# Attention over the prompt: where the next keys stand between the scores and the turn of two other heads

## The chip, the core and the metric

The kernel runs on one core of a Trainium2 chip. The metric is the device time of one execution in microseconds. A core has a matrix engine (TensorE, PE in the rows; its loads of weights are listed apart as PEld), a vector engine (VectorE, DVE), a scalar engine (ScalarE, ACT), GpSimd (POOL) and SyncE (SP), which here issues nearly all transfers. Each engine works through its own queue in order, and the engines wait for each other on semaphores.

## What is computed

One step of a two-layer streaming encoder trunk over a prompt of 256 frames and 8 running streams of 16 frames each. Layer 0 mixes by multi-head latent attention, layer 1 by retention; each has a half feed-forward block before and behind. The change lies in the attention of layer 0 over the prompt, 8 heads:

```python
def mla_prompt(h, pos, w_dq, q_norm, w_uq, w_dkv, kv_norm, w_uk, w_uv, w_o):
    q_nope, q_pe, ckv, kpe = mla_project(...)
    k_nope = jnp.einsum('bkl,lhn->bkhn', ckv, w_uk)          # keys
    v = jnp.einsum('bkl,lhv->bkhv', ckv, w_uv)               # values
    for blk in range(s // QBLK):                             # 2 blocks of 128 queries
        q0 = blk * QBLK
        kend = q0 + QBLK
        sc = (jnp.einsum('bqhn,bkhn->bhqk', q_nope[:, q0:kend], k_nope[:, :kend])
              + jnp.einsum('bqhr,bkr->bhqk', q_pe[:, q0:kend], kpe[:, :kend]))
        ...
        p = jax.nn.softmax(jnp.where(mask, sc, -jnp.inf), axis=-1).astype(v.dtype)
        outs.append(jnp.einsum('bhqk,bkhv->bqhv', p, v[:, :kend]))
```

## The kernel before, in words

The program is a row of phases: feed-forward, attention, feed-forward, feed-forward, retention, feed-forward, end. The feed-forward blocks and projections multiply in three terms with weights split into a high and a low part (L167 to L169); they hold most of the time.

In the attention phase the prompt part is written out by hand, once for each engine. What sets the order is only the order of the calls in `pe_prompt` (TensorE) and `act` (ScalarE), and what `dve` does per head; semaphores then hold an engine at the head of its queue. For head h the steps are:

- `keys(h)`: TensorE, two products into a bank (L928); ScalarE copies them to `kn` (L1150), two buffers.
- `scores(h)`: TensorE, four products into bank `up_ps[h % 2]` (L944, L945), for two blocks of 128 queries with 128 and 256 keys.
- VectorE takes the row maxima (L1322) and negates them (L1326); ScalarE's `exps(h)` writes `pr` (L1171, in the rows `cc`, whose memory it shares); VectorE inverts the sums (L1333) and scales `pr` (L1338).
- `turn(h)`: TensorE, three transposes of `pr` into `down_ps[h % 2]` (L956); ScalarE's `turned(h)` copies them to `prT` (L1162, in the rows `mtab`).
- `mix(h)`: TensorE, values by `prT` (L969), which waits for that copy; ScalarE's `mixed(h)` copies the result to `XH` (L1154), and VectorE keeps the rest in `XL` (L1312).
- `sample_queries(n)`, n = 0 to 3: TensorE, eight small products for the running streams (L985); ScalarE copies each to `lat` in two instructions (L1141).

In the steady loop TensorE works through turn(h), keys(h+3), mix(h), scores(h+2), turn(h+1), and so on. ScalarE's queue is keys, mixed, turned, exps in each pass. In the passes i = 2 and 3 ScalarE and VectorE also split a half of a weight tile (L152, L160). Behind the prompt part comes that of the running streams (`sample_scores`, L1035 and L1039, and `pe_sample`), and then the output projection.

Of the kernel before, what the change touches and what calls it, by code (L numbers as in the profile page):

```python
# [15 lines left out]
MLA_HEADS, NOPE, ROPE, Q_LORA, KV_LORA = D_MODEL // 128, 128, 64, 3 * D_MODEL // 8, D_MODEL // 4  # L16
# [30 lines left out]
def stream_kernel(nc, a, out):  # L47

    ctx = ExitStack()
    with ctx:  # L50
# [13 lines left out]
        def sem(name):  # L64

            if name not in sems:
                sems[name] = ctx.enter_context(nc.semaphore(name))
            return sems[name]
# [684 lines left out]
        class Mla:  # L753
# [146 lines left out]
            def pe_prompt(self, pe):  # L900
# [3 lines left out]
                def values(i):  # L904
                    kt_, half = i // 2, i % 2
                    if i >= 2:
                        pe.wait_ge(sem("m_proj"), (15, 18)[i - 2])
                    for t in range(KV):
                        pe.wait_ge(sem("m_ckvT"), t + 1)
                        mm = pe.matmul(self.VAL_BANKS[i][:, 0:512], ckvT[:, t, kt_ * P:(kt_ + 1) * P],  # L910
                                       wuv[:, t, half * 512:(half + 1) * 512], start=(t == 0), stop=(t == KV - 1))
                    mm.then_inc(sem("m_val"), 1)
# [7 lines left out]
                def keys(h):  # L920
                    if h == 0:
                        pe.wait_ge(sem("wuk_in"), 16)
                    if h < 2:
                        pe.wait_ge(sem("m_proj"), (13, 16)[h])
                    else:
                        pe.wait_ge(sem("m_kn"), h - 1)
                    for t in range(KV):
                        mm = pe.matmul(gate_ps[1 - h % 2][:, 0:SEQ], wuk[:, t, h * P:(h + 1) * P], ckvT[:, t, 0:SEQ],  # L928
                                       start=(t == 0), stop=(t == KV - 1))
                    mm.then_inc(sem("m_keys"), 1)  # L930

                def scores(h):
                    pe.wait_ge(sem("m_kn"), h + 1)
                    if h % 2 == 0:
                        pe.wait_ge(sem("m_rope"), 3 + 3 * (h // 2 + 1))
                    if h < 2:
                        pe.wait_ge(sem("m_proj"), (17, 14)[h])
                    else:
                        pe.wait_ge(sem("m_exp"), 2 * (h - 1))
                    ps = up_ps[h % 2]  # L940
                    at = 0
                    for blk in range(NP):
                        n, q0 = (blk + 1) * QBLK, blk * QBLK
                        pe.matmul(ps[:, at:at + n], qn[:, h, q0:q0 + QBLK], kn[:, h % 2, 0:n], start=True, stop=False)  # L944
                        mm = pe.matmul(ps[:, at:at + n], qp[:, h, q0:q0 + QBLK], kpT[:, 0:n], start=False, stop=True)  # L945
                        at += n
                    mm.then_inc(sem("m_scores"), 1)

                def turn(h):
                    pe.wait_ge(sem("m_pr"), 2 * (h + 1))  # L950
                    if h < 2:
                        pe.wait_ge(sem("m_val_out"), (4, 3)[h])
                    else:
                        pe.wait_ge(sem("m_prT"), h - 1)
                    for i in range(SC // P):
                        mm = pe.transpose(down_ps[h % 2][:, i * P:(i + 1) * P], pr[:, h % 2, i * P:(i + 1) * P], ident[:, :])  # L956
                    mm.then_inc(sem("m_prTurned"), 1)

                def mix(h):
                    ps = (norm_ps, misc_ps)[h % 2]  # L960
                    pe.wait_ge(sem("m_prT"), h + 1)
                    if h == 0:
                        pe.wait_ge(sem("m_val_out"), 4)
                    if h >= 2:
                        pe.wait_ge(sem("m_ol"), h - 1)
                    at = 0
                    for blk in range(NP):
                        for k in range(blk + 1):
                            mm = pe.matmul(ps[:, blk * QBLK:(blk + 1) * QBLK], val[:, k, h * P:(h + 1) * P],  # L969
                                           prT[:, h % 2, at:at + P], start=(k == 0), stop=(k == blk))  # L970
                            at += P
                    mm.then_inc(sem("m_mixed"), 1)

                def sample_queries(i):

                    ps = gate_ps[i % 2]
                    if i == 0:
                        pe.wait_ge(sem("m_kn"), MLA_HEADS)
                        pe.wait_ge(sem("wukT_in"), 16)
                    if i >= 2:  # L980
                        pe.wait_ge(sem("m_lat"), KV * (i - 1))
                    for t in range(KV):
                        for e in range(2):
                            h = 2 * i + e
                            mm = pe.matmul(ps[:, (t * 2 + e) * P:(t * 2 + e + 1) * P], wukT[:, h, t * P:(t + 1) * P],  # L985
                                           qn[:, h, SEQ:T], start=True, stop=True)
                    mm.then_inc(sem("m_qlat"), 1)
# [5 lines left out]
                keys(1)  # L993
                scores(0)
                values(3)
                for i in range(2, MLA_HEADS + 1):
                    if i < MLA_HEADS:
                        keys(i)
                    else:
                        sample_queries(0)  # L1000
                        sample_queries(1)
                    if i >= 3:
                        mix(i - 3)
                    scores(i - 1)
                    turn(i - 2)
                sample_queries(2)
                sample_queries(3)
                mix(MLA_HEADS - 2)
                turn(MLA_HEADS - 1)
                self.sample_scores(pe, 0)  # L1010
# [81 lines left out]
            def act(self, act):  # L1092
# [35 lines left out]
                def value_tile(i):  # L1128
                    act.wait_ge(sem("m_val"), i + 1)
                    act.activation(val[:, i // 2, (i % 2) * 512:(i % 2 + 1) * 512], self.VAL_BANKS[i][:, :], ACT.Copy)\  # L1130
                        .then_inc(sem("m_val_out"), 1)
# [5 lines left out]
                def sample_queries(i):  # L1137
                    act.wait_ge(sem("m_qlat"), i + 1)
                    ps = gate_ps[i % 2]
                    for t in range(KV):  # L1140
                        act.activation(lat[:, t, :, 2 * i:2 * i + 2, :].rearrange("p b e q -> p e b q"),  # L1141
                                       ps[:, t * 2 * P:(t + 1) * 2 * P].rearrange("p (e b q) -> p e b q", e=2, b=DEC_BATCH),
                                       ACT.Copy).then_inc(sem("m_lat"), 1)


                def keys(h):
                    act.wait_ge(sem("m_keys"), h + 1)
                    if h >= 2:
                        act.wait_ge(sem("m_scores"), h - 1)
                    act.activation(kn[:, h % 2, :], gate_ps[1 - h % 2][:, 0:SEQ], ACT.Copy).then_inc(sem("m_kn"), 1)  # L1150

                def mixed(h):
                    act.wait_ge(sem("m_mixed"), h + 1)
                    act.activation(XH[:, h, 0:SEQ], (norm_ps, misc_ps)[h % 2][:, 0:SEQ], ACT.Copy).then_inc(sem("m_oh"), 1)  # L1154

                def turned(h):
                    act.wait_ge(sem("m_prTurned"), h + 1)
                    if h == 0:
                        act.wait_ge(sem("m_rope"), 3 + 3 * 4)
                    if h >= 2:  # L1160
                        act.wait_ge(sem("m_mixed"), h - 1)
                    act.activation(prT[:, h % 2, :], down_ps[h % 2][:, 0:SC], ACT.Copy).then_inc(sem("m_prT"), 1)  # L1162
# [18 lines left out]
                exps(0)  # L1181
                value_tile(2)
                value_tile(3)
                for i in range(2, MLA_HEADS + 1):
                    if i < MLA_HEADS:
                        keys(i)
                    else:
                        sample_queries(0)
                        sample_queries(1)
                    if i >= 3:  # L1190
                        mixed(i - 3)
                    turned(i - 2)
                    exps(i - 1)
                    if i < 4:
                        c = self.c0 + 8
                        part_hi(act, c, c % 2, c // 2, i % 2)
                sample_queries(2)
                sample_queries(3)
                mixed(MLA_HEADS - 2)
                turned(MLA_HEADS - 1)  # L1200
                mixed(MLA_HEADS - 1)
# [968 lines left out]
```

## Time and profile before

| | |
|---|---|
| time, three runs | 1614.07 us median (1613.97 to 1615.7) |
| the profiled execution's own time | 1614.1 us |
| its span, first to last instruction | 1611.9 us |
| TensorE busy | 1601.0 us, 99% of the span |
| TensorE weight loads busy | 1535.7 us, 95% |
| VectorE busy | 822.2 us, 51% |
| ScalarE busy | 597.8 us, 37% |
| GpSimd busy | 262.7 us, 16% |
| mean granted TensorE clock | 0.999 of full speed |

A product's recorded duration overlaps that of the next, since products are pipelined: what one costs the path is the distance from its start to the start of the next. The loop that is changed runs from about 338 to 362 us of the span. Around the span lie 1614.1 - 1611.9 = 2.2 us.

### The profile page before, as it was taken

To read this page: it belongs to the slowest core of one execution; us is meant where nothing else is said; L and a number is where in the kernel's file an instruction comes from. 1 tells how busy PE (TensorE), PEld (TensorE's weight loads), DVE (VectorE), ACT (ScalarE), POOL (GpSimd) and SP (SyncE) were. 2 spreads that over 40 slices of the span, in tenths; PEclk is the share of its full clock that TensorE was granted. 3 is DMA by queue.
4 is the path that set the end of the run, shared out by engine and by line. 5 is a ranking of instruction groups with operands and counts; after the bars stand their busy time and mean duration, and the time that the engine had idled before them with its cause. 6 is when DMAs were issued, how large, how long until landed. Compare 5 with 4: busy or idle time off the path is not lost.

```text
span 1611.9 us, 24112 instructions
## 1 busy us (share of the span) xinstructions
PE 1601.0 (99%) x9170; PEld 1535.7 (95%) x9170; DVE 822.2 (51%) x968; ACT 597.8 (37%) x770; POOL 262.7 (16%) x250
## 2 busy tenths in 40 slices
PE   9999999999999999999999999999999999999998
PEld 9999999989999999999999999798989899999987
DVE  6544344864454444445444344675747486444422
ACT  6333322574343332234333323424243354333322
POOL 0111122631121110221111032202020202111000
PEclk9999999999999999999999999999999999999999
DMA  7444344554244443454444345566574755444332
GB/s 219 123 120 128 110 128 128 177 185 163 63 121 130 130 130 97 127 141 131 130 130 122 108 126 191 189 227 224 199 252 167 260 182 144 130 130 130 113 125 102
DMA packets 323440, 239.07 MB, mean 148 GB/s; under 512 B 9216, under 2 KB 287936, under 8 KB 323264
## 3 DMA queue, kind: packets, MB, share of 16 engines
q1 hardware_dynamic: 322960, 237.92, 48.3%
q8 instruction: 32, 0.52, 0.1%
q10 hardware_dynamic: 432, 0.50, 0.1%
q14 instruction: 16, 0.13, 0.0%
HBM read 215.34 MB, written 20.94 MB: 147 GB/s over the span
## 4 chain that ended last, share of the span: by engine, by line
PE 95%; SPq 2%; ACT 1%; DMA 1%; DVE 1%; issue 0%; ACTq 0%
PE bank L167 26%; PE bank L168 26%; PE bank L169 26%; PE bank L488 2%; PE bank L489 2%; PE bank L487 2%; SPq L1568 2%; PE bank L1067 1%; PE bank L396 1%; PE bank L1653 1%; PE bank L1655 1%; PE bank L1654 1%; PE bank L1763 1%; PE bank L1035 1%; PE bank L1722 1%; PE bank L1039 1%
## 5 line engine op out<-in xcount | busy, mean ns | idle before, releaser
L144 DVE TENSOR_TENSOR WL<-RAW,WH 128x2048 fp32r<-128x2048 f32 (+3 forms) x191 | 402.7, 2110 | 289.6 <-ACT WH L137 288.8
L137 ACT ACTIVATE WH<-RAW 128x2048 fp32r<-128x2048 f32 (+3 forms) x191 | 330.0, 1730 | 565.3 <-PE bank L169 478.1
L167 PE MATMUL bank<-XH,WH 128*128 128x384 f32 x1376 | 461.1, 335 | 0.0
L169 PE MATMUL bank<-XH,WL 128*128 128x384 f32 x1376 | 459.8, 334 | 0.0
L168 PE MATMUL bank<-XL,WH 128*128 128x384 f32 x1376 | 459.7, 334 | 0.0
L167 PEld LDWEIGHTS bank<-XH,WH 128*128 128x128 f32 x1376 | 258.3, 188 | 3.4 <-issue 2.0
L168 PEld LDWEIGHTS bank<-XL,WH 128*128 128x128 f32 x1376 | 258.3, 188 | 0.2
L169 PEld LDWEIGHTS bank<-XH,WL 128*128 128x128 f32 x1376 | 258.3, 188 | 0.0
L653 POOL TENSOR_TENSOR si<-si,rsb 128x384 f32<-128x384 f32 x88 | 94.7, 1076 | 625.5 <-ACT si L524 591.1
L167 PE MATMUL bank<-AH,WH 128*128 128x384 f32 x528 | 176.4, 334 | 0.0
L168 PE MATMUL bank<-AL,WH 128*128 128x384 f32 x528 | 176.4, 334 | 0.0
L169 PE MATMUL bank<-AH,WL 128*128 128x384 f32 x528 | 176.4, 334 | 0.0
L584 DVE TENSOR_TENSOR au<-bank,si 128x384 f32<-128x384 f32 x86 | 48.0, 558 | 250.0 <-PE bank L169 232.4
L524 ACT ACTIVATE si<-gs 128x384 f32<-128x384 f32 x86 | 45.2, 525 | 229.1 <-DVE gs L576 229.1
L167 PE MATMUL bank<-X2H,WH 128*128 128x384 f32 x344 | 114.9, 334 | 0.0
L169 PE MATMUL bank<-X2H,WL 128*128 128x384 f32 x344 | 114.9, 334 | 0.0
L168 PE MATMUL bank<-X2L,WH 128*128 128x384 f32 x344 | 114.9, 334 | 0.0
L167 PEld LDWEIGHTS bank<-AH,WH 128*128 128x128 f32 x528 | 99.1, 188 | 0.0
L168 PEld LDWEIGHTS bank<-AL,WH 128*128 128x128 f32 x528 | 99.1, 188 | 0.0
L169 PEld LDWEIGHTS bank<-AH,WL 128*128 128x128 f32 x528 | 99.1, 188 | 0.0
L167 PEld LDWEIGHTS bank<-X2H,WH 128*128 128x128 f32 x344 | 64.6, 188 | 0.1
L168 PEld LDWEIGHTS bank<-X2L,WH 128*128 128x128 f32 x344 | 64.6, 188 | 0.0
(282 smaller groups left out, 1938.0 us busy)
## 6 DMA issues: line engine op xcount, KB each, us to landing
RAW<-w_ffn_gate_dram SPq DMA_DIRECT2D x86, 512.0 KB, 3.9
RAW<-w_ffn_up_dram SPq DMA_DIRECT2D x86, 512.0 KB, 5.1
RAW<-w_ret_in_dram SPq DMA_DIRECT2D x48, 512.0 KB, 4.6
RAW<-w_ffn_down_dram SPq DMA_DIRECT2D x48, 384.0 KB, 4.0
st<-state_ret_dram SPq DMA_DIRECT2D x32, 512.0 KB, 6.9
new_state_sample_dram<-st SPq DMA_DIRECT2D x32, 512.0 KB, 6.5
RAW<-w_ffn_down_dram SPq DMA_DIRECT2D x48, 320.0 KB, 3.4
RAW<-w_ffn_down_dram SPq DMA_DIRECT2D x22, 512.0 KB, 3.9
```

The lines of the kernel that those rows point to most:

```text
L137: ins = act.activation(dst(WH), src, ACT.Copy)
L144: ins = dve.tensor_tensor(dst(WL), src, dst(WH).bitcast(F32), ALU.subtract)
L167: pe.matmul(ps, wh, xh, start=first, stop=False)
L168: pe.matmul(ps, wh, xl, start=False, stop=False)
L169: return pe.matmul(ps, wl, xh, start=False, stop=last)
L487: pe.matmul(ps[:, :], ah, wh, start=False, stop=False)
L488: pe.matmul(ps[:, :], ah, wl, start=False, stop=False)
L489: mm = pe.matmul(ps[:, :], al, wh, start=False, stop=(stop and f == 1))
L524: act.activation(si[:, j, :], gs[:, j, :], ACT.Silu).then_inc(self.silu_done, 1)
L584: dve.tensor_tensor(au[:, j, :], up_ps[j][:, 0:T], si[:, j, :], ALU.mult).then_inc(self.act_done, 1)
L653: pool.tensor_tensor(si[:, j, :], si[:, j, :], rsb[:, 0:T], ALU.mult).then_inc(self.silu_scaled, 1)
L1568: sp.dma_start(vp[row:row + DEC_SEQ, odd, :], src).then_inc(sem("r_vd_in"), 16)
```

## The change

In both queues the keys of head i+1 are now made in pass i, behind scores(i-1) and ahead of turn(i-2), where they had stood at the start of pass i+1, behind turn(i-2). keys(2) moves out of the loop and keeps its place. The sample queries, which take the place of the keys at the end, move in the same way: 0 and 1 go ahead of turn(5), 2 and 3 ahead of turn(6). Waits, buffers, instructions and transfers are the same; the line numbers behind the change fall by one or two.

```diff
@@ pe_prompt @@
                 scores(0)
                 values(3)
+                keys(2)
                 for i in range(2, MLA_HEADS + 1):
-                    if i < MLA_HEADS:
-                        keys(i)
-                    else:
-                        sample_queries(0)
-                        sample_queries(1)
                     if i >= 3:
                         mix(i - 3)
                     scores(i - 1)
+                    if i + 1 < MLA_HEADS:
+                        keys(i + 1)
+                    else:
+                        for n in (0, 1) if i < MLA_HEADS else (2, 3):
+                            sample_queries(n)
                     turn(i - 2)
-                sample_queries(2)
-                sample_queries(3)
                 mix(MLA_HEADS - 2)
                 turn(MLA_HEADS - 1)
@@ act @@
                 value_tile(3)
+                keys(2)
                 for i in range(2, MLA_HEADS + 1):
-                    if i < MLA_HEADS:
-                        keys(i)
-                    else:
-                        sample_queries(0)
-                        sample_queries(1)
                     if i >= 3:
                         mixed(i - 3)
+                    if i + 1 < MLA_HEADS:
+                        keys(i + 1)
+                    else:
+                        for n in (0, 1) if i < MLA_HEADS else (2, 3):
+                            sample_queries(n)
                     turned(i - 2)
                     exps(i - 1)
                     if i < 4:
                         c = self.c0 + 8
                         part_hi(act, c, c % 2, c // 2, i % 2)
-                sample_queries(2)
-                sample_queries(3)
                 mixed(MLA_HEADS - 2)
                 turned(MLA_HEADS - 1)
```

TensorE in one pass of the loop: L944 and L945 are the scores, L928 the keys, L956 the turn, L969 the mix.

```order
 L944 MATMUL bank<-kn,shared 128x256
 L945 MATMUL bank<-kall,qp 128x256
+L928 MATMUL bank<-kall,shared 128x256 x2
 L956 MATMUL bank<-ident,cc 128x128 x3
-L928 MATMUL bank<-kall,shared 128x256 x2
 L969 MATMUL bank<-mtab,val 128x128 x3
 L944 MATMUL bank<-kn,shared 128x128
```

The keys moved from behind the turn to ahead of it, so that the mix now follows the turn of the same head. Five passes look like this.

TensorE in the last pass, with the sample queries (L985) in the place of the keys:

```order
 L944 MATMUL bank<-kn,shared 128x256
 L945 MATMUL bank<-kall,qp 128x256
+L985 MATMUL bank<-shared,wukT 128x128 x8
 L956 MATMUL bank<-ident,cc 128x128 x3
-L985 MATMUL bank<-shared,wukT 128x128 x8
 L969 MATMUL bank<-mtab,val 128x128 x3
 L956 MATMUL bank<-ident,cc 128x128 x3
```

Two passes have them: turn(5) and mix(5), turn(6) and mix(6) now stand side by side, and turn(7) comes right behind mix(6).

ScalarE between two turns, before (L1171 the exponentials, L1150 the keys, L1154 the mix, L1162 the turn):

```order
L1171 ACTIVATE cc,stat<-bank,stat 128x128
L1171 ACTIVATE cc,stat<-bank,stat 128x256
L1150 ACTIVATE kn<-bank 128x256
L1154 ACTIVATE XH<-bank 128x256
L1162 ACTIVATE mtab<-bank 128x384
```

and with the change, where the same lines are one lower:

```order
L1170 ACTIVATE cc,stat<-bank,stat 128x128
L1170 ACTIVATE cc,stat<-bank,stat 128x256
L1153 ACTIVATE XH<-bank 128x256
L1149 ACTIVATE kn<-bank 128x256
L1161 ACTIVATE mtab<-bank 128x384
```

The copy of the keys now stands between the copy of the mix and that of the turn; it is that of a head one higher.

## Rows read from the trace of the kernel before

**Rows 1.** The page: the chain that ended last, shares by engine.

```profile
PE 95%; SPq 2%; ACT 1%; DMA 1%; DVE 1%; issue 0%; ACTq 0%
```

**Rows 2.** The chain between 402 and 1020 us, shares by line.

```profile
by line: PE bank L168 31.9%; PE bank L167 31.9%; PE bank L169 31.8%; PE bank L1067 0.7%; PE bank L1087 0.6%; PE bank L1653 0.5%; PE bank L1654 0.5%; PE bank L425 0.4%; PE bank L423 0.4%; PE bank L430 0.4%; PE bank L1655 0.4%; PE bank L220 0
```

**Rows 3.** TensorE timeline: start us, us, line, operands, records [idle before <-releaser].

```profile
344.76 0.49 PE L956 MATMUL bank<-ident,cc 128*128 128x128 f32 x3
345.09 1.03 PE L928 MATMUL bank<-kall,shared 128*128 128x256 f32 x4
345.95 0.83 PE L969 MATMUL bank<-mtab,val 128*128 128x128 f32 x6
346.62 0.39 PE L944 MATMUL bank<-kn,shared 128*128 128x128 f32 x2
...
347.07 0.60 PE L944 MATMUL bank<-kn,shared 128*128 128x256 f32 x2
347.50 0.59 PE L945 MATMUL bank<-kall,qp 128*128 128x256 f32 x2
348.12 0.55 PE L956 MATMUL bank<-ident,cc 128*128 128x128 f32 x3
```

**Rows 4.** TensorE timeline, around the turn of head 1.

```profile
340.74 0.59 PE L945 MATMUL bank<-kall,qp 128*128 128x256 f32 x2
341.53 0.55 PE L956 MATMUL bank<-ident,cc 128*128 128x128 f32 x3 [0.20 <-DVE cc L1338]
```

**Rows 5.** VectorE timeline, the scaling of head 1.

```profile
340.21 1.27 DVE L1338 TENSOR_SCALAR cc<-cc,stat 128x128 f32<-128x128 f32 x2
```

**Rows 6.** ScalarE timeline, around the turn of head 3.

```profile
345.29 0.49 ACT L1162 ACTIVATE mtab<-bank 128x384 f32<-128x384 f32 x1 [0.20 <-PE bank L956]
...
348.71 0.49 ACT L1162 ACTIVATE mtab<-bank 128x384 f32<-128x384 f32 x1 [0.93 <-PE bank L956]
349.17 0.37 ACT L1171 ACTIVATE cc<-bank,stat 128x128 f32<-128x128 f32 x1
...
349.98 0.38 ACT L1150 ACTIVATE kn<-bank 128x256 f32<-128x256 f32 x1
350.24 0.39 ACT L1154 ACTIVATE XH<-bank 128x256 fp32r<-128x256 f32 x1
```

**Rows 7.** VectorE timeline, the end of head 4 and the start of head 5.

```profile
350.12 0.17 DVE L1333 RECIPROCAL stat<-stat 128x2 f32<-128x2 f32 x1 [0.98 <-ACT cc L1171]
350.32 0.55 DVE L1338 TENSOR_SCALAR cc<-cc,stat 128x128 f32<-128x128 f32 x2
...
351.56 0.62 DVE L1322 TENSOR_REDUCE stat<-bank 128x1 f32<-128x128 f32 x2 [0.36 <-PE bank L945]
352.21 0.17 DVE L1326 TENSOR_SCALAR stat<-stat 128x2 f32<-128x2 f32 x1
```

**Rows 8.** TensorE timeline, the end of the loop.

```profile
358.95 1.95 PE L985 MATMUL bank<-shared,wukT 128*128 128x128 f32 x16
360.74 0.83 PE L969 MATMUL bank<-mtab,val 128*128 128x128 f32 x6
361.46 0.55 PE L956 MATMUL bank<-ident,cc 128*128 128x128 f32 x3
361.95 1.16 PE L1035 MATMUL bank<-kt,lat 128*128 128x272 f32 x4
```

**Rows 9.** ScalarE timeline, the copies of sample queries 2 and 3.

```profile
360.49 1.20 ACT L1141 ACTIVATE lat<-bank 128x256 f32<-128x256 f32 x4
```

**Rows 10.** Waits between 325 and 368 us: total us, times, longest us.

```profile
ACT mtab L1162 <- PE bank L956: 6.7, 7, 1.3
```

**Rows 11.** Stretches: start:end, us, busy time of each engine, PEclk, DMA share, GB/s.

```profile
338.00:342.00 4.00, 3.80 (x26) 3.18 (x25) 2.73 (x8) 2.89 (x8) 3.50 (x5) 1.00 0.00 0
1041.00:1043.00 2.00, 0.97 (x11) 0.34 (x9) 0.73 (x2) 1.72 (x4) 0.00 (x0) 1.00 0.00 1
...
1605.00:1612.00 7.00, 1.62 (x8) 1.00 (x6) 1.32 (x3) 1.70 (x4) 0.00 (x0) 0.76 0.38 150
```

## The prediction, made before the changed kernel had run

> **What bounds the kernel now.** I read the page's chain first: 95% of the span is TensorE's own work [rows 1]. Then the same chain over the stretch behind the change, 402 to 1020 us: apart from a fraction of a per cent every share is TensorE's [rows 2], so a delay of TensorE in the attention is not made up before the retention phase. What counts is therefore each slot that TensorE loses between 338 and 362 us. For that I read TensorE's timeline there. A pass holds turn, keys, mix and scores without a gap: the starts 344.76, 345.09, 345.95, 346.62 and, a pair later than 347.50, 347.93 give slots of 0.33, 0.86, 0.67 and 1.31 us, 3.17 in all (the last pair's slot is 347.50 - 347.07 = 0.43) [rows 3]. Two turns start later than their slot: that of head 1 at 341.53 where 340.74 + 0.43 = 341.17 was due, 0.36 late, released by VectorE, whose scaling took 1.27 instead of 0.55 us [rows 4, 5, 7]; and that of head 4 at 348.12 where 347.93 was due, 0.19 late [rows 3]. All that the change could win in the loop is there.
>
> **Part 1: keys ahead of the turn, the waits of turns.** Five turns (heads 0 to 4) start one keys slot, 0.86 us, later behind their scores. Both late turns had lacked less than that, so both waits go. A turn that had waited also takes 0.55 instead of 0.49 us for its three transposes [rows 3, 4]: I book 0.06 for each restart. Gain: 0.36 + 0.19 + 2 x 0.06 = 0.67 us. At the end of the loop the turn of head 7 stands at 361.46 where 360.74 + 0.67 = 361.41 was due, and the product behind it starts 0.49 instead of 0.33 behind it [rows 8]: it waits for the sample queries' last copy, 360.49 + 1.20 = 361.69 [rows 9]. That copy comes earlier now; gain 0.05 + 0.16 + 0.06, some 0.27. Together 0.94 us.
>
> **Part 2: the mix right behind its own turn.** mix(h) multiplies what ScalarE copied out of turn(h)'s bank. Before, the keys' 0.86 us lay between them and hid the copy. The profile shows how closely: a turn starting at 344.76 lets the copy start at 345.29, 0.53 later (0.59 where the turn had itself waited: 348.12 to 348.71), and the copy takes 0.49 [rows 3, 6]. Released 0.04 later, as VectorE's end at 340.21 + 1.27 = 341.48 releases the turn at 341.53 [rows 4, 5], the mix could start 0.53 + 0.49 + 0.04 = 1.06 us behind the turn's start. It was due at 0.33 + 0.86 = 1.19: free by 0.13. Now it is due at 0.33: TensorE waits 0.73, and restarts for 0.06. This price needs the copy to start at once. Ahead of it in ScalarE's queue is now the copy of the keys, which end 0.17 behind their slot's end; it starts 0.21 after the turn has started, and a queued successor starts 0.26 later (349.98 to 350.24) [rows 6], at 0.47, just ahead of the turn's 0.53. So nothing is added; bound: its whole 0.38 instead of 0.26 would add 0.06 a pass. Heads 0 to 4: 5 x 0.79 = 3.95 us.
>
> All copies of turns had waited for the transposes (7 of them, 6.7 us [rows 10]), so ScalarE had room, and the copy cannot come sooner than the turn.
>
> **Part 3: the sample queries ahead of turns 5 and 6.** Let s be the end of the scores' slot. Two sample queries hold TensorE (360.74 - 358.95) = 1.79 us, 0.89 each, and the turn then stands at s + 1.79 and ends its slot at s + 2.12 [rows 8]. ScalarE must first copy both: four instructions in 1.20, some 0.28 apart [rows 9]. The second query's results are there at s + 1.95, its two copies hold the queue from 1.99 to 2.55; the turn's copy then runs to 3.04 and the mix starts at s + 3.08. TensorE waits 0.96, with restart 1.02. Twice: 2.04 us.
>
> **Part 4: the turn of head 7.** Behind mix(6) it needs the probabilities of head 7. exps(7) is queued behind those four copies and turned(6): it starts at s + 3.08, and from the start of the exponentials to the end of VectorE's scaling lie 350.32 + 0.55 - 349.17 = 1.70 us [rows 6, 7]. So the turn can start at s + 4.82; mix(6) has ended its slot at 3.08 + 0.06 + 0.67 = 3.81. Wait 1.01, with restart 1.07. Before, 1.79 us of sample queries covered this.
>
> **Who else is held.** In each pass the exponentials move behind a later turned copy: from the scores' end, negated maxima are ready at about 1.0 (0.21 + 0.65 + 0.17 [rows 7]), exponentials start at 1.92, probabilities stand at 3.62. The next turn is now due at 0.86 + 0.33 + 0.79 + 0.67 + 1.31 + 0.86 = 4.82, so 1.2 us are spare: a scaling of 1.27 us fits. VectorE's half splits of a weight tile in passes 2 and 3 stand behind the maxima and end ahead of the exponentials; they end perhaps 1 to 2 us later in time. Behind them SP loads weights and the cached latents, which had long landed when used; its order is the same, and I book nothing. GpSimd's work is that of before, and the running streams' part follows with its own spacings.
>
> **The sum.** 3.95 + 2.04 + 1.07 - 0.94 = 6.12 us. On the profiled execution's own 1614.1 us, which is the runs' median within 0.1, that gives **1620.2 us**, 0.38% slower; the span becomes 1618.0. Bounds of unknown terms: without any restart cost 8 x 0.06 = 0.5 less; with the keys' copy at full length and a release of 0.1 instead of 0.04, 0.3 + 0.5 more; the whole sum between 5.3 and 7.2.
>
> The Trainium skill, "TensorE: Matmul & The Clock Gate", section "Architectural detail: the array is 16× 32×32, not 1× 128×128", says that TensorE can pull a load of weights ahead of products still in flight. The weights of a mix are the values, long in place. If loads pass a waiting product too, the restart cost falls away, and by that rule the sum would be 5.6. The trace speaks against leaning on it: turns that had waited took 0.55 and not 0.49 us [rows 3, 4].
>
> **Rivals.** *The delay is made up later (no change).* The chain has 5% that isn't TensorE, most of it in retention [rows 1], where TensorE stood still once for 1.03 of 2 us [rows 11]. If what is waited for there had been started by something that the attention doesn't delay, up to all 6.1 us would vanish: 1614.1. It decides at the first wait behind 1020 us. Against it: loads there follow the use of earlier tiles, which TensorE sets. 7%. *The turns' waits are all that moves (ends on the other side).* If the mix of a head didn't have to wait, because the copy of turn(h) were complete within the turn's 0.33 us slot, only the 0.94 us gain would stay: 1613.2, faster than before, but within 0.2%. The copy alone takes 0.49 [rows 6]. 2%. *The softmax becomes the bound in each pass.* If ScalarE's queue slipped by over 1.2 us a pass, turns 1 to 6 would wait as well; each 0.5 us past that point costs 3 us: some 1624. Only the half splits could do that, in two passes. 3%. *The clock falls.* TensorE would stand still for some 0.7 of every 4 us. In the last 7 us of the span, with 1.62 us busy, the granted clock is 0.76, a mix of its two levels; over the 1 us of standing still in retention, and over the late turn of head 1, it stays 1.00 [rows 11]. At 1.2 GHz instead of 2.4 seven passes of 3.17 us would take as long again: 1642. 3%. The Trainium skill, same page, section "Part 1: The HAM clock gate", ties the half clock to a matrix engine that has been idle. The trace agrees at its end (0.76) and shows no loss over 1 us of standing still (1.00) [rows 11].
>
> **The numbers.** Forecast 85%, made up later 7%, only a gain 2%, softmax 3%, clock 3%. About 0.2% (3.2 us) is what a measurement of this kernel can tell from no change. Slower by more: 85 + 3 + 3 = 91%; the other 9% lie about no change, 7 within the bound and 2 below it, since the small gain and a scatter of the runs can add up. The runs of before lie up to 1.6 us above their lowest, so I widen the sum's 5.3 to 7.2 to 1618.4 to 1621.9; the rivals outside it hold less than 2 in 10.
>
> **What would show it.** Right: in TensorE's timeline a gap of about 0.7 us ahead of L969 in the passes of heads 0 to 4, released by ScalarE's copy of the turn, 0.9 to 1.0 for heads 5 and 6, and about 1 us ahead of the turn of head 7, released by VectorE's scaling; no gap ahead of other turns; passes of 3.95 us; the granted clock at 1.00; the end of the loop some 6 us later, and the same distance at the end of the span. Wrong: mixes without a gap (part 2 falls), turns that still wait (part 1), gaps much beyond 0.8 (ScalarE's queue holds the copy), or a span that grows by less than the loop.

## The result, and the profile after

The changed kernel takes 1622.0 us in the median of 6 runs (1620.39 to 1623.12). The kernel before, with three more runs beside these, takes 1615.76 us (1613.97 to 1616.05). The ratio is 1.004, 95% interval 1.003 to 1.0051: slower by 6.2 us. The forecast difference was 6.1 us; the forecast time, 1620.2, is 1.8 us too low, and the median lies 0.1 us outside the range. The profiled execution took 1622.35 us, with a span of 1620.1.

TensorE's timeline in a pass of the loop, heads 1 and 2 (it answers to [rows 3]; columns are start, duration, engine, line, operands, records, idle before and who ended it):

```profile
344.62 0.49 PE L956 MATMUL bank<-ident,cc 128*128 128x128 f32 x3
345.69 0.94 PE L969 MATMUL bank<-mtab,val 128*128 128x128 f32 x6 [0.58 <-ACT mtab L1161]
346.47 0.39 PE L944 MATMUL bank<-kn,shared 128*128 128x128 f32 x2
...
347.78 1.03 PE L928 MATMUL bank<-kall,shared 128*128 128x256 f32 x4
348.64 0.49 PE L956 MATMUL bank<-ident,cc 128*128 128x128 f32 x3
349.71 0.94 PE L969 MATMUL bank<-mtab,val 128*128 128x128 f32 x6 [0.58 <-ACT mtab L1161]
```

The mix starts 1.07 us behind the start of its turn; the turn needs a slot of 0.33, so 0.74 are lost. (The row says 0.58, since a recorded duration runs on past the slot.) The mix then holds 346.47 - 345.69 = 0.78 us, where it held 0.67 before: a restart costs 0.11. A pass is 4.02 us, 3.17 before. No turn of heads 0 to 6 waits.

The same pass on ScalarE (it answers to [rows 6]):

```profile
344.82 0.38 ACT L1149 ACTIVATE kn<-bank 128x256 f32<-128x256 f32 x1 [1.18 <-PE bank L928]
345.15 0.49 ACT L1161 ACTIVATE mtab<-bank 128x384 f32<-128x384 f32 x1
345.54 0.36 ACT L1170 ACTIVATE cc<-bank,stat 128x128 f32<-128x128 f32 x1
```

The copy of the turn starts at 345.15, 0.53 behind the turn's start, as before, and ends at 345.64; the mix follows at 345.69. The keys' copy ahead of it costs nothing. The exponentials, with their maxima long there, start 0.39 behind the copy's start and not behind its end.

The end of the loop on TensorE (it answers to [rows 8]):

```profile
365.00 1.95 PE L985 MATMUL bank<-shared,wukT 128*128 128x128 f32 x16
366.78 0.49 PE L956 MATMUL bank<-ident,cc 128*128 128x128 f32 x3
368.08 0.94 PE L969 MATMUL bank<-mtab,val 128*128 128x128 f32 x6 [0.80 <-ACT mtab L1161]
369.66 0.55 PE L956 MATMUL bank<-ident,cc 128*128 128x128 f32 x3 [0.65 <-DVE cc L1336]
370.04 1.08 PE L1034 MATMUL bank<-kt,lat 128*128 128x272 f32 x4
```

mix(6) starts 1.30 behind its turn, 0.97 more than the slot, and the turn of head 7 starts 0.80 late (368.08 + 0.78 = 368.86 was due). What TensorE's products waited for between 334 and 378 us, in total, times and longest:

```profile
PE bank L969 <- ACT mtab L1161: 4.5, 7, 0.8
PE bank L956 <- DVE cc L1336: 0.6, 1, 0.6
```

Seven waits for a copy and one for a scaling are all there is.

**Where the rest of the difference lies.** To measure the loop apart from the rest I take the distance from the last pair of head 1's scores (L945) to the turning of the new rows (L917). Before it is 337.57 to 368.03, 30.46 us; with the change it is:

```profile
339.31 0.59 PE L945 MATMUL bank<-kall,qp 128*128 128x256 f32 x2
...
376.06 0.38 PE L917 MATMUL bank<-ident,kall 128*128 128x128 f32 x2
```

36.75 us, 6.29 more. But the two spans differ by 1620.1 - 1611.9 = 8.2. The loop already starts 1.74 later. The chain that ended last shows where that arises; before:

```profile
5.92 16.88 PE bank L396 x96
```

and after:

```profile
5.89 18.63 PE bank L396 x96
```

The first 96 products behind the warming ones (products of ones by ones, with which TensorE starts) take 1.75 us longer, in code that the change doesn't touch. Whether that belongs to the change was the first open question.

### The profile page after: what moved, and what is told of

Same layout as the page of the kernel before. It is cut to its first block, busy times and chain, and to the rows that moved or that the text cites. A ratio compares the mean times of both kernels' runs of the same rounds, so it can differ in the third digit from the quotient of the medians.

```text
span 1620.1 us, 24112 instructions
## 1 busy us (share of the span) xinstructions
PE 1604.2 (99%) x9170; PEld 1538.2 (95%) x9170; DVE 821.5 (51%) x968; ACT 598.1 (37%) x770; POOL 262.6 (16%) x250
## 4 chain that ended last, share of the span: by engine, by line
PE 94%; SPq 2%; ACT 2%; DMA 1%; issue 1%; DVE 1%; ACTq 0%
PE bank L167 25%; PE bank L169 25%; PE bank L168 25%; PE bank L487 2%; PE bank L488 2%; PE bank L489 2%; SPq L1566 2%; PE bank L396 1%; PE bank L1066 1%; PE bank L1651 1%; PE bank L1653 1%; PE bank L1652 1%; PE bank L1761 1%; PE bank L1034 1%; PE bank L1720 1%
```

## The experiments

Theory A has two parts: in the loop, each mix waits for the copy of its own turn, to the amount that the work between them doesn't cover; and the 1.75 us at the start come and go in executions of either kernel. The rivals stand with each run. All distances are those of the loop as above.

| kernel | loop, us | against before | L396 chain, us | profiled time, us |
|---|---|---|---|---|
| before | 30.46 | | 16.88 | 1614.1 |
| changed | 36.75 | +6.29 | 18.63 | 1622.35 |
| keys only | 34.03 | +3.57 | 16.88 | 1617.55 |
| queries only | 33.18 | +2.72 | 18.96 | 1619.01 |
| keys, half behind the turn | 31.87 | +1.41 | 16.88 | 1615.41 |
| mix behind the next scores | 29.71 | -0.75 | 18.82 | 1615.94 |
| the same, 14 warming products | 29.70 | -0.76 | 16.88 | 1614.16 |
| before, 14 warming products | 30.47 | +0.01 | 16.73 | 1614.5 |
| changed, 14 warming products | 36.74 | +6.28 | 16.66 | 1623.31 |

### Keys alone

```diff
+                keys(2)
                 for i in range(2, MLA_HEADS + 1):
-                    if i < MLA_HEADS:
-                        keys(i)
-                    else:
+                    if i == MLA_HEADS:
                         sample_queries(0)
                         sample_queries(1)
                     if i >= 3:
                         mix(i - 3)
                     scores(i - 1)
+                    if i + 1 < MLA_HEADS:
+                        keys(i + 1)
                     turn(i - 2)
```

and the same in ScalarE's order.

> Only the keys are moved ahead of the turns of heads 0 to 4; the sample queries stay where they were. Theory A (each mix waits for its own turn's copy): five gaps ahead of a mix, 0.84 us each with the slower restart, less the two turn waits of 0.67: the loop is 3.5 us longer than before (33.98 us from the last pair of head 1's scores to L917, against 30.46), the time about 1614.0 + 3.5 or 1615.8 + 3.5. Theory B (most of the 6.3 us is the end of the loop, where exponentials queue behind the sample queries' copies): under 2 us here.

Measured: 34.03 us, 3.57 more than before; median 1619.21 us, ratio 1.0025 (1.0016 to 1.0035). TensorE's products wait five times:

```profile
PE bank L969 <- ACT mtab L1163: 2.9, 5, 0.6
```

5 x (0.74 + 0.11) - 0.67 = 3.58. Theory A holds to a tenth; theory B falls.

### Sample queries alone

```diff
                     if i < MLA_HEADS:
                         keys(i)
-                    else:
-                        sample_queries(0)
-                        sample_queries(1)
...
                     scores(i - 1)
+                    if i >= MLA_HEADS - 1:
+                        for n in (0, 1) if i < MLA_HEADS else (2, 3):
+                            sample_queries(n)
                     turn(i - 2)
-                sample_queries(2)
-                sample_queries(3)
```

and the same on ScalarE.

> Only the sample queries are moved ahead of turns 5 and 6; the keys stay where they were. Theory A: 2 gaps of 1.07 us ahead of mix 5 and 6 and one of 0.86 ahead of turn 7, less 0.27 that was lost at the loop's end: 2.7 us longer than before (33.2 us over the same distance), with the turns of heads 1 and 4 still 0.36 and 0.19 late. Together with the keys alone it makes the whole change, 6.3. Theory B: over 4 us here.

Measured: 33.18 us, 2.72 more; median 1618.76 us, ratio 1.002 (1.001 to 1.003). The two parts add up to the whole, 3.57 + 2.72 = 6.29. The turn of head 1 waits as it did before (it answers to [rows 4]):

```profile
342.71 0.59 PE L945 MATMUL bank<-kall,qp 128*128 128x256 f32 x2
343.51 0.55 PE L956 MATMUL bank<-ident,cc 128*128 128x128 f32 x3 [0.21 <-DVE cc L1334]
```

### Half of the cover given back

A head's keys are two products. One stays ahead of the turn, one goes behind it; ScalarE's order is that of before.

```diff
                     scores(i - 1)
+                    if i + 1 < MLA_HEADS:
+                        keys(i + 1)
                     turn(i - 2)
+                    if i + 1 < MLA_HEADS:
+                        key_part(i + 1, 1)
```

Here `keys(h)` for h of 3 and more holds only the first product.

> The keys of a head are two products of 0.43 us. One stands ahead of the turn, as in the change, and one behind it, as before; ScalarE's order and the sample queries are those of before. Theory A: the copy of a turn is ready 1.07 us behind the turn's start and the mix is due at 0.33 + 0.43 = 0.76, so five gaps of some 0.3 us with 0.1 for the slower restart; both turn waits (0.36, 0.19) still go: 5 x 0.41 - 0.67 = 1.4 us over the 30.46 of before, 31.9 us. Rival (the gap comes from the order of ScalarE's copies, not from the cover): no gap, 29.8 us, since ScalarE's order is that of before.

Measured: 31.87 us, 1.41 more, median 1616.37 us, ratio 1.0011 (1.0002 to 1.002). One pass:

```profile
342.15 0.49 PE L961 MATMUL bank<-ident,cc 128*128 128x128 f32 x3
342.48 0.60 PE L932 MATMUL bank<-kall,shared 128*128 128x256 f32 x2
343.22 0.94 PE L974 MATMUL bank<-mtab,val 128*128 128x128 f32 x6
```

The mix starts 1.07 behind its turn again, whatever stands between: 0.33 + 0.43 are used, 0.31 lost. Five times 0.31 + 0.11, less 0.67, are 1.43. No bracket stands behind the mix, because the recorded duration of the key product covers most of the gap (342.48 + 0.60 = 343.08); the starts show it. With ScalarE's order of before the gap is still there, so it isn't that order.

### The mix behind the next scores

The change's order of keys and turn is kept, and each mix moves one place further back. Sample queries 1, 2 and 3 go back behind their turn, and VectorE takes the low part of a mix later. The diff is against the changed kernel, with ScalarE's part, which moves the sample queries in the same way, left out.

```diff
                 for i in range(2, MLA_HEADS + 1):
+                    scores(i - 1)
                     if i >= 3:
                         mix(i - 3)
-                    scores(i - 1)
                     if i + 1 < MLA_HEADS:
                         keys(i + 1)
-                    else:
-                        for n in (0, 1) if i < MLA_HEADS else (2, 3):
-                            sample_queries(n)
+                    elif i < MLA_HEADS:
+                        sample_queries(0)
                     turn(i - 2)
+                    if i == MLA_HEADS - 1:
+                        sample_queries(1)
+                sample_queries(2)
+                sample_queries(3)
...
                 for h in range(MLA_HEADS):
-                    if h >= 2:
-                        mixed_lo(h - 2)
                     dve.wait_ge(sem("m_scores"), h + 1)
...
                         part_lo(dve, c0 + 8, (c0 + 8) % 2, 1, h - 2)
+                    if h >= 2:
+                        mixed_lo(h - 2)
                     dve.wait_ge(sem("m_exp"), 2 * (h + 1))
```

> The keys stay ahead of the turn as in the change, but each mix moves behind the scores of the next head but one, so that 1.31 us of scores lie between a turn and its mix; the last passes keep sample queries 1, 2 and 3 behind their turn, and the low part of a mix is made behind the negated maxima. Theory A (only the missing cover costs): no gap ahead of any mix and none ahead of a turn: 0.5 to 0.9 us shorter than before over the same distance, 29.6 to 30.0 us, time the same as before. Rival (keys ahead of the turn cost by themselves, through ScalarE's queue): still 2 us or more longer than before.

Measured: 29.71 us, 0.75 less than before:

```profile
341.24 0.49 PE L956 MATMUL bank<-ident,cc 128*128 128x128 f32 x3
341.56 0.39 PE L944 MATMUL bank<-kn,shared 128*128 128x128 f32 x2
...
342.88 0.83 PE L969 MATMUL bank<-mtab,val 128*128 128x128 f32 x6
343.54 1.03 PE L928 MATMUL bank<-kall,shared 128*128 128x256 f32 x4
344.41 0.49 PE L956 MATMUL bank<-ident,cc 128*128 128x128 f32 x3
```

With the scores between turn and mix nothing waits, and a pass is back at 344.41 - 341.24 = 3.17 us. So keys ahead of the turn don't cost by themselves: once the copy is covered, the loop is shorter than before. The 0.75 us lie near the forecast's gain of 0.94 (0.67 of it for the turns' waits), but this order differs from that of before in more than the keys, so the gain isn't shown to be theirs alone. The median is 1614.95 us against 1615.25, ratio 0.9995 (0.9985 to 1.0005): a gain that the trace shows and the times don't resolve.

### The start of the span

> The kernel before, unchanged, for a second profile. The changed kernel's span grew by 8.2 us, of which only 6.3 lie in the attention's loop; 1.75 lie in the first 96 products of the span (L396), which took 18.63 us there against 16.88 in the first profile of before. Theory A (the first dozen products run at half the clock in some executions, of either kernel): the times of this kernel fall into two groups, near 1614.0 and near 1615.8, and the L396 chain takes either about 16.9 or about 18.6 us, with the distance from the scores of head 1 to the turning of the new rows (L917) at 30.46 us either way. Theory B (the 1.75 us belong to the change, through another placing of the code): all profiles of this kernel show 16.9.

The first further profile of the kernel before had 16.88 us again, with a loop of 30.47; its times were 1613.99 to 1616.55. That told nothing apart; three more followed.

> The kernel before once more, for a profile of an execution with a slow start. Both profiles of it so far have L396 at 16.88 us and lie near 1614.0. Theory A: an execution near 1615.8 shows L396 at 18.6 to 19.0 us with 30.46 us in the loop; one near 1614.0 shows 16.9. Theory C (another place, the retention for instance, makes the second group): near 1615.8 with L396 at 16.9.

> A further execution of the kernel before: either near 1614.0 with L396 at 16.9 us, or near 1615.8 with 18.6 to 19.0 (Theory A).

> A further execution of the kernel before: either near 1614.0 with L396 at 16.9 us, or near 1615.8 with 18.6 to 19.0 (Theory A); the loop's distance stays 30.46 us.

The second and the fourth had 16.88 us, at 1614.32 and 1614.55. The third took 1616.0 us, with the same loop (30.46), and its chain reads:

```profile
5.88 18.65 PE bank L396 x96
```

So the kernel before has this start as well; that it belongs to the change falls. The first products of this third one:

```profile
5.88 1.62 PE L396 MATMUL bank<-XH,WH 128*128 128x384 f32 x4 [1.10 <-DVE XH L312]
7.30 1.48 PE L396 MATMUL bank<-XH,WL 128*128 128x384 f32 x4
8.58 1.38 PE L396 MATMUL bank<-XL,WH 128*128 128x384 f32 x4
9.80 0.86 PE L396 MATMUL bank<-XH,WH 128*128 128x384 f32 x4
```

The first four take 1.42 us from start to start, the next four 1.28, 0.32 each, and later ones stand 0.173 apart (the whole chain of 96 in 16.88 is 0.176 each). About the first twelve are slow, behind an idle of 1.10 us. I read it as the lower of the two levels of TensorE's clock, 1.2 and 2.4 GHz, though 0.32 is 1.85 times 0.173 and not twice; but the granted clock doesn't show it. The same stretch of 6 to 8 us (columns as in [rows 11]) in the first profile of before, with the short start:

```profile
6.00:8.00 2.00, 2.00 (x12) 2.00 (x13) 2.00 (x4) 1.01 (x2) 0.00 (x0) 1.00 0.97 300
```

and in the first of the changed kernel, with the long one:

```profile
6.00:8.00 2.00, 2.00 (x7) 2.00 (x8) 2.00 (x4) 0.99 (x2) 0.00 (x0) 1.00 1.01 348
```

7 products in place of 12, and both rows give a granted clock of 1.00 (the column behind the engines). Two other profiles bear on it. In the kernel before with 14 warming products (below), these stand 0.213 us apart up to 4.3 us of the span and 0.112 from there, and the granted clock is 1.00 on both sides, so this column doesn't tell the two rates apart here:

```profile
3.00:4.00 1.00, 1.00 (x7) 1.00 (x6) 0.00 (x0) 0.00 (x0) 0.00 (x0) 1.00 1.00 317
4.00:5.00 1.00, 1.00 (x10) 1.00 (x10) 0.00 (x0) 0.63 (x1) 0.00 (x0) 1.00 1.07 364
```

And in a place of the changed kernel with 14 warming products where the granted clock does fall, to 0.53, products of the same shape stand 0.32 apart, as here; the rows are at the end of this section.

### The changed kernel once more

> The changed kernel again: 36.75 us over the loop's distance. With L396 at 16.9 us its time is near 1620.4 (Theory A), with 18.6 to 19.0 near 1622.2. Its difference to a profile of before with the same L396 is 6.2 to 6.5 us.

Measured: loop 36.74, L396 16.90, time 1621.51 us: the loop and the start as expected, the time 1.1 too long. The lost time is in the retention phase. Its waits of TensorE between 960 and 1330 us:

```profile
PE bank L1720 <- ACT on L1851: 3.0, 3, 1.6
PE bank L1651 <- DVE WL L144: 0.6, 1, 0.6
PE bank L1720 <- issue: 0.6, 1, 0.6
```

and those of the first profile of the changed kernel:

```profile
PE bank L1720 <- ACT on L1851: 2.6, 3, 1.3
PE bank L1720 <- issue: 0.6, 1, 0.6
```

So a second place differs between executions: the wait behind a round of small transfers near 1040 us, here with one for a low part of a weight tile near 1018 us. The 0.4 us more of the one and the 0.6 of the other make up most of the 1.1. In the five profiles of before the three waits of the first line sum to 2.2 to 2.6.

### More warming products

```diff
-            for _ in range(8):
+            for _ in range(14):
                 pe.matmul(misc_ps[:, 0:P], ones[:, :], ones[:, :], start=True, stop=True)
```

in the kernel before, in that with the later mix, and in the changed one.

> The kernel before with 14 instead of 8 warming products ahead of the first real one, so that TensorE is busy until about 6 us instead of standing still from 4.8. Theory A (the first dozen real products run at half rate in some executions because the clock isn't up): the L396 chain takes 16.9 us in the profile, and the times lie close together near 1614, without the group near 1616; where the warming products themselves run at half rate to the end, the first real product starts up to 1 us later. Rival (the 1.75 us are something else, transfers for instance): the same spread as before, 1613.9 to 1618.

> The mix moved behind the scores (0.75 us shorter than before in the loop) with the 14 warming products. Theory A: near 1613.3, lower than both kernels, 29.7 us over the loop's distance. Rival: 1614.9, as with the moved mix alone.

> The changed kernel with the 14 warming products. Theory A: 36.75 us over the loop's distance as without them, L396 at 16.9 us, times near 1614.0 + 6.3 = 1620.3 with little spread. Rival: 1620.4 to 1623.1 as before.

The profiles have L396 at 16.73, 16.88 and 16.66 us and loops of 30.47, 29.70 and 36.74, as expected. The times do not follow. The kernel before with 14 warming products has 1615.45 us (1614.5 to 1618.09) against 1614.83, ratio 1.0002 (0.9993 to 1.0011). With the later mix it has 1615.0, ratio 1.0001 (0.9992 to 1.001), and the changed kernel, in 4 runs, 1623.02 (1621.86 to 1623.78), where 1620.3 was expected. Part of the cause is in all three profiles, a wait in the retention phase that grew. In the kernel before with warming products:

```profile
PE bank L1722 <- ACT on L1853: 1.8, 3, 0.8
PE bank L1722 <- issue: 1.7, 1, 1.7
```

"issue" means that no other engine is waited for. It is 1.3 to 1.7 us with the six products more and 0.5 or 0.6 in every profile without them. So something outside the loop changes with the six products; what it is no run here tells.

In the changed kernel with warming products more is lost right behind that wait. There the granted clock falls (columns as in [rows 11]):

```profile
1300.00:1302.00 2.00, 0.81 (x9) 0.47 (x10) 0.12 (x2) 1.96 (x5) 0.00 (x0) 1.00 0.00 0
1302.00:1304.00 2.00, 2.00 (x8) 2.00 (x9) 2.00 (x4) 1.97 (x3) 0.00 (x0) 0.61 0.00 0
1304.00:1306.00 2.00, 2.00 (x8) 2.00 (x8) 0.70 (x2) 0.08 (x1) 0.00 (x0) 0.53 0.00 0
```

and the products go at the distance of the slow start, 0.32:

```profile
1303.46 0.53 PE L167 MATMUL bank<-XH,WH 128*128 128x384 f32 x1
1303.78 0.53 PE L168 MATMUL bank<-XL,WH 128*128 128x384 f32 x1
```

Set beside the third further profile of before, product by product, this costs some 1.6 us between 1301 and 1306 us, in one of the three profiles with 14 warming products: an idle of 1.69 us went before it there, and one of 1.7 us in the kernel before, where the products behind it keep 0.173. The 1.1 us by which the wait grew and these 1.6 make up most of the way from the expected 1620.3 to the profile's 1623.31.

Whether the six products take the slow start away in every execution stays open too, since their profiles show one execution each, and the spread didn't shrink. No version here beats the kernel before by an amount that the runs resolve.

## Why the prediction was right or wrong

**What bounds the kernel, and whether the delay stays.** Right. In a pair of profiles with the same start, the changed kernel's 1620.1 and the third further profile of before, 1613.7 (L396 at 18.63 and 18.65), the spans differ by 6.4 us, the loops by 6.29. Nothing behind the loop gives it back; that rival falls. The 0.1 more lies at the wait behind the small transfers, 2.6 us in the one and 2.5 in the other.

**Part 1, the turns' waits.** Right. The two late turns no longer wait. They are those of heads 1 and 3: the turn at 348.12, which the prediction calls that of head 4, is turn(3), and with the change it starts at 352.66, where 351.80 + 0.86 was due. The product behind turn(7) starts 0.38 behind it, where it was 0.49. That it had waited for the sample queries' copy isn't shown: it had started 0.26 behind the end of that copy, where the other releases here took 0.04 to 0.05.

**Part 2, the mix right behind its turn.** Right in mechanism and in the 1.06 us, measured 1.07. The restart was mis-sized: 0.11 a time and not 0.06. The 0.06 was read from transposes that had waited [rows 3, 4], and a mix is not a transpose. Five passes cost 4.25 us and not 3.95. The prediction had weighed a case in which the restart cost falls away. It began from a rule of the Trainium skill on pulled weight loads ("TensorE: Matmul & The Clock Gate", section "Architectural detail: the array is 16× 32×32, not 1× 128×128"), which speaks of loads ahead of products still in flight. That loads also pass a product that waits for a copy was the prediction's own step, and here they don't. The weights of the mix had long been there, and the wait for the copy stands ahead of both in the program; their loads stood still as long as the products:

```profile
345.69 0.74 PEld L969 LDWEIGHTS bank<-mtab,val 128*128 128x128 f32 x6 [0.82 <-ACT mtab L1161]
```

**Part 3, the sample queries.** Right. Mixes 5 and 6 start 1.29 and 1.30 behind their turns, as worked out (3.08 - 1.79). With the longer restart that is 0.96 + 0.97 + 2 x 0.11 = 2.15 and not 2.04.

**Part 4, the turn of head 7.** The mechanism held, the size was too large: 0.80 + 0.06 = 0.86, forecast 1.07. I had the exponentials wait for the end of the turn's copy (0.49 + 0.04). They only stand behind it in the queue and start 0.37 behind its start, which is 0.16 of the 0.21 us that the wait was too large; the other 0.05 is the restart of mix(6), which ends that much later:

```profile
367.53 0.50 ACT L1161 ACTIVATE mtab<-bank 128x384 f32<-128x384 f32 x1
367.90 0.38 ACT L1170 ACTIVATE cc<-bank,stat 128x128 f32<-128x128 f32 x1
```

The terms as measured, with the gain as forecast, are 4.25 + 2.15 + 0.86 - 0.94 = 6.32, beside 6.29 for the loop and a forecast of 6.12. That the sum came out so close is in part luck: the restarts were too small by 0.41 and part 4 too large by 0.21.

**Who else is held, and the rivals.** The softmax didn't become the bound in the passes: their turns don't wait. Head 2's scaling ends 1.4 us ahead of its turn at 348.64, where 1.2 had been worked out:

```profile
346.68 0.55 DVE L1336 TENSOR_SCALAR cc<-cc,stat 128x128 f32<-128x128 f32 x2
```

The clock doesn't fall there either. It is granted at 1.00 over the loop, where TensorE stands still for 0.7 of every 4 us, and the products keep their distances of full rate:

```profile
346.00:350.00 4.00, 3.42 (x23) 2.93 (x22) 2.97 (x8) 2.82 (x9) 0.00 (x0) 1.00 0.00 0
```

The copy can't be had within the turn's slot: it starts 0.53 behind the turn's start, where the slot is 0.33.

**The numbers: the step that failed.** "On the profiled execution's own 1614.1 us, which is the runs' median within 0.1." The difference was right, 6.1 forecast and 6.2 measured, and the base was not: with more runs the median of before is 1615.76, 1.7 us above the level that I added to. Added to that, the forecast would have been 1621.9. Later comparisons have the kernel before at 1615.25 and 1614.83.

Three runs had given 1613.97, 1614.07 and 1615.7, and I read the third as scatter around the first two. In the comparison with 27 runs of the kernel before, 14 lie at 1614.21 to 1614.83 and 13 at 1615.68 to 1616.83, with none between (in that with 31, on another chip, the gap is filled). The one profile in the upper group's stretch, at 1616.0, shows the slow start, and the four at 1613.99 to 1614.55 don't. The third run itself wasn't profiled; that it had the slow start fits its time and isn't shown. Of the changed kernel, the two shortest runs, 1620.39 and 1620.42, lie at the forecast 1620.2; the other four lie at 1621.95 and above. So the forecast met the fastest executions, and the median is made of others too. The slow start isn't their only cause: the further profile of the changed kernel had the short start and took 1621.51, and the runs with 14 warming products spread as widely.

The range went wrong with the base. The terms named for the sum's bounds give 5.6 and 6.9; the rest of "between 5.3 and 7.2" had none. The range ended 0.6 us above 1614.1 + 7.2 = 1621.3. It should have carried the full 1.6 us by which the third run lay above the median (1.7 above the lowest run, which is what the prediction's 1.6 was said to be).

## What to carry to other kernels

Between a product and the product that reads a copy of its result there must stand as much work as copy and hand-overs take, here 1.07 us from start to start. Moving that work ahead of the first product takes it away from there, even if the wait for which it was moved is gone; move the reader back too, and both are covered. And a forecast of a difference of 0.4% needs the level of the base from more than one execution: look in the trace of each for a place outside the change that differs.

## What was not expected of the hardware

- The first 12 to 14 products behind the warming ones stood 0.32 us apart (0.46 behind the first) and then 0.173, in 4 of the 11 profiles with 8 warming products (changed, sample queries alone, later mix, before), while the granted clock's row says 1.00. It costs 1.75 to 2.1 us.
- A group of six products that had waited held TensorE 0.11 us longer than one that follows without a gap (0.78 and 0.67), a group of three transposes 0.06 (0.39 and 0.33).
- With six more products at the start of TensorE's stream, a wait with no releaser near 1300 us took 1.3 to 1.7 us in 3 of 3 profiles, and 0.5 or 0.6 in the 11 without them. Behind one of these waits the granted clock fell to 0.53, and some 1.6 us more were lost.
